# Local attention in a hybrid decoder kernel: values stationary in two column halves, normalised probabilities streamed, the result born transposed

## The chip, the cores and the metric

The program runs on one core of a Trainium2 chip. Its time is the device time of one execution in microseconds (us); the time given for a kernel is the median of its runs. The engines are TensorE (PE for matmuls, PEld for the loads of its stationary operand), VectorE (DVE), ScalarE (ACT), GpSimd (POOL) and SyncE (SP, which here only issues DMAs).

## The reference, cut to what matters

Two layers; each is half a feed-forward block, a mixing block with three branches, and half a feed-forward block. All is f32. The branch that is changed is the sliding-window attention: 256 tokens in two blocks of 128, 16 query heads of 64 columns, 2 key/value heads.

```python
def sliding_window_attention(q, k, v, sinks):
    ...
    s = jnp.einsum('bnqkgd,bnskd->bnkgqs', qb, kk,
                   preferred_element_type=jnp.float32) * (hd ** -0.5)
    ...
    m = jnp.maximum(jnp.max(s, axis=-1, keepdims=True), sink)
    p = jnp.exp(s - m)
    p = p / (jnp.sum(p, axis=-1, keepdims=True) + jnp.exp(sink - m))
    o = jnp.einsum('bnkgqs,bnskd->bnqkgd', p.astype(v.dtype), vv)
    return o.reshape(B, S, H * hd)
```

The result is multiplied with `w_up_swa` (1024 x 1024), gated and added to the other two branches.

## The kernel before, in words

Weights come from HBM in units of 1 MB (128 partitions x 2048 f32). A unit lands in a raw buffer; ACT rounds it to a high part `w_hi` (line 1171), DVE subtracts to get the low part `w_lo` (line 1566), and PE multiplies in three passes, low-high, high-high and high-low (lines 763 to 765), 24 matmuls of 512 columns for a unit. There are three slots of `w_hi`/`w_lo` (`RING`), so ACT may split a unit only when PE is through with the one three items back. Some matrices are multiplied in pairs with a scheme of seven block products (`rk:5`, `rg:1` and so on, 12 matmuls each), for which sums of weight quarters are made either by DVE (line 1563, "raw") or by a DMA of POOL that adds on landing (line 700, table `ADDED`).

The order of everything in the mixing block is one list, `SCHEDULE`, and all engines walk it. `mk0.1` is a unit, `rk:5` a block product, the rest are steps. Those of the local attention, for each group `g` of four heads: `s0` to `s3` (scores; PE line 971, then on DVE scale, mask and maximum, lines 1828 to 1839), `e0` to `e3` (exponentials and row sums on ACT, line 1472), `pt0` to `pt3` (12 transposes of probabilities on PE, line 983, copied out by ACT to `pT`, line 1397), `pv0` to `pv3` (probabilities times values). In `pv` the transposed probabilities are stationary and the values, 64 columns, stream (lines 995 and 997); the result is token-major, and DVE divides it by the row sums on its way to the buffer `stA` (line 1853). When all four groups are there, `st` transposes `stA` (16 transposes, line 820), and ACT and DVE make the high and low parts `bT_hi` and `bT_lo` of it (lines 1188 and 1584). These are the stationary operand of the units `us0.0` to `us1.1`.

Raw buffers: three of their own; `raw_x` in the place of `x` while `x` is parked in HBM; and in the mixing block `raw_b`, two units in the place of `bT_hi`/`bT_lo`, from behind the `mv` units until `st` (constant `B_ITEMS`).

PE takes a matmul with f32 operands as two records in the trace (16 for the 8 score matmuls of a group, 24 for the 12 value matmuls). `prob` holds two groups at a time.

Of the kernel before, what the change touches and what calls it, by code (L numbers as in the profile page):

```python
# [189 lines left out]
RAW_B, RAW_Q, RAW_X = (3, 4), (5, 6), 7  # L190
X_ITEMS = AT[0]["mix", UNIT_AT["mk1", 0]] + 4, AT[0]["mix", UNIT_AT["wo0", 0]] - 6
_st = STEPS.index(("step", "st"))
_after_st = next(s for s in STEPS[_st:] if s[0] != "step")
B_ITEMS = (max(AT[0]["mix", UNIT_AT[c, 1]] for c in ("mv0", "mv1")) + 5,
           AT[0][_after_st if _after_st[0] == "prod" else ("mix", _after_st[1])] + 1)
# [104 lines left out]
def plan_banks(l):  # L300
# [38 lines left out]
    sizes |= {f"pt{g}": (3, False) for g in range(NGRP)} | {f"pv{g}": (1, False) for g in range(NGRP)}  # L339
# [1670 lines left out]
```

## Time and profile before

| what | value |
|---|---|
| median of 3 runs | 1453.86 us (1453.58 to 1456.06) |
| the profiled execution's own time | 1452.88 us |
| its span, first to last instruction | 1451.1 us |
| PE busy in the span | 1431.3 us (99%), 6814 matmuls |
| DVE busy | 1162.2 us (80%) |
| ACT busy | 977.7 us (67%) |

The profiled execution took 1452.88 us, 1.8 us more than its span, and 1.0 us less than the median. A busy time counts a matmul from its start to its modelled end, and neighbours overlap; what a matmul costs is therefore read as the distance between two starts.

### The profile page before, as it was taken

The numbers are of one execution on the slowest core, as the hardware profiler recorded it, in microseconds if no ns is written. First come the engines' busy times: TensorE is split into PE (matmuls) and PEld (weight loads), VectorE is DVE, ScalarE is ACT, GpSimd is POOL, SyncE is SP. The second block draws the span as 40 slices with busy tenths as digits, with TensorE's granted clock in tenths as the row PEclk, the third lists the DMA queues.
The fourth block names the chain that finished last, engine by engine and source line by source line (L and its number), as shares of the span: only waits on it lengthen the run. The fifth ranks groups of instructions, "written<-read, shape, count | busy, mean of one in ns | idle before, by whom it ended". The sixth has DMA issues, their size and how long they took to land.

```text
span 1451.1 us, 17969 instructions
## 1 busy us (share of the span) xinstructions
PE 1431.3 (99%) x6814; PEld 1186.6 (82%) x6814; DVE 1162.2 (80%) x1322; ACT 977.7 (67%) x1430; POOL 67.9 (5%) x93
## 2 busy tenths in 40 slices
PE   8999999999999999999999999999999999999997
PEld 6887888888888888888888778888888888888885
DVE  7999756798768768898798986468987778689985
ACT  6777666769756647676577775668696666576763
POOL 0000000000000000000000000000000000000000
PEclk9999999999999999999999999999999999999999
DMA  9998738775668777788849776467865787768871
GB/s 367 267 291 236 276 130 276 243 232 178 173 221 262 219 301 245 238 281 250 300 144 279 251 214 250 196 208 265 234 171 196 229 246 232 307 198 267 259 233 44
DMA packets 49397, 341.42 MB, mean 235 GB/s; under 512 B 5568, under 2 KB 6208, under 8 KB 8608
## 3 DMA queue, kind: packets, MB, share of 16 engines
q1 hardware_dynamic: 37392, 259.54, 47.5%
q0 software_dynamic: 8912, 63.84, 22.9%
q10 hardware_dynamic: 3008, 16.90, 2.9%
q8 instruction: 55, 0.90, 0.2%
q14 instruction: 30, 0.25, 0.0%
HBM read 332.91 MB, written 7.34 MB: 234 GB/s over the span
## 4 chain that ended last, share of the span: by engine, by line
PE 83%; DVE 10%; DMA 3%; issue 2%; ACT 1%; SPq 0%; POOLq 0%; POOL 0%; DVEq 0%; ACTq 0%
PE bank L763 25%; PE bank L765 24%; PE bank L764 24%; DVE w_lo L1566 5%; PE bank L820 3%; DMA raw_b<-in_stream 3%; DVE w_lo_more L1566 2%; PE bank L997 1%; PE bank L1098 1%; PE bank L1080 1%; PE bank L971 1%; PE bank L983 1%; DMA raw<-in_stream 1%; DVE raw L1563 1%; PE bank L995 0%
## 5 line engine op out<-in xcount | busy, mean ns | idle before, releaser
L1566 DVE TENSOR_TENSOR w_lo<-raw,w_hi 128x1024 fp32r<-128x1024 f32 x342 | 402.3, 1219 | 133.4 <-ACT w_hi L1171 133.2
L1171 ACT ACTIVATE w_hi<-raw 128x1024 fp32r<-128x1024 f32 x342 | 342.9, 1053 | 168.2 <-PE bank L765 136.1
L763 PE MATMUL bank<-w_hi,hT_lo 128*128 128x512 f32 (+1 forms) x696 | 274.3, 394 | 2.7 <-DVE half L1669 1.9
L765 PE MATMUL bank<-w_lo,hT_hi 128*128 128x512 f32 (+1 forms) x696 | 268.3, 386 | 0.0
L764 PE MATMUL bank<-w_hi,hT_hi 128*128 128x512 f32 (+1 forms) x696 | 267.9, 385 | 0.0
L763 PEld LDWEIGHTS bank<-w_hi,hT_lo 128*128 128x128 f32 x696 | 130.9, 188 | 32.1 <-DVE half L1669 2.8
L765 PEld LDWEIGHTS bank<-w_lo,hT_hi 128*128 128x128 f32 x696 | 130.8, 188 | 26.7
L764 PEld LDWEIGHTS bank<-w_hi,hT_hi 128*128 128x128 f32 x696 | 131.1, 188 | 24.4
L763 PE MATMUL bank<-w_hi,S_lo 128*128 128x512 f32 x364 | 144.9, 398 | 1.3 <-ACT snap L1252 0.9
L765 PE MATMUL bank<-w_lo,S_hi 128*128 128x512 f32 x364 | 142.1, 390 | 0.0
L764 PE MATMUL bank<-w_hi,S_hi 128*128 128x512 f32 x364 | 141.9, 390 | 0.0
L1566 DVE TENSOR_TENSOR w_lo<-raw_b,w_hi 128x1024 fp32r<-128x1024 f32 x96 | 113.0, 1217 | 21.4 <-ACT w_hi L1171 21.2
L763 PE MATMUL bank<-w_hi,bT_lo 128*128 128x512 f32 x320 | 125.5, 392 | 0.0
L765 PE MATMUL bank<-w_lo,bT_hi 128*128 128x512 f32 x320 | 124.7, 390 | 0.0
L764 PE MATMUL bank<-w_hi,bT_hi 128*128 128x512 f32 x320 | 124.6, 389 | 0.0
L1171 ACT ACTIVATE w_hi<-raw_b 128x1024 fp32r<-128x1024 f32 x96 | 96.3, 1055 | 36.0 <-PE bank L765 24.5
L763 PE MATMUL bank<-w_hi,gT_lo 128*128 128x512 f32 x240 | 94.5, 394 | 3.6 <-DVE gT_lo L1584 3.5
L765 PE MATMUL bank<-w_lo,gT_hi 128*128 128x512 f32 x240 | 93.6, 390 | 0.0
L764 PE MATMUL bank<-w_hi,gT_hi 128*128 128x512 f32 x240 | 93.5, 389 | 0.0
L1566 DVE TENSOR_TENSOR w_lo<-raw_q,w_hi 128x1024 fp32r<-128x1024 f32 x72 | 84.7, 1218 | 4.6 <-ACT w_hi L1171 4.5
L1171 ACT ACTIVATE w_hi<-raw_q 128x1024 fp32r<-128x1024 f32 x72 | 72.3, 1056 | 15.8 <-PE bank L765 12.3
L763 PEld LDWEIGHTS bank<-w_hi,S_lo 128*128 128x128 f32 x364 | 68.4, 188 | 17.7 <-ACT snap L1252 1.6
(227 smaller groups left out, 2436.3 us busy)
## 6 DMA issues: line engine op xcount, KB each, us to landing
raw<-in_stream SPq DMA_DIRECT2D x150, 1024.0 KB, 6.1
raw_b<-in_stream SPq DMA_DIRECT2D x38, 1024.0 KB, 6.7
raw_q<-in_stream SPq DMA_DIRECT2D x38, 1024.0 KB, 6.9
raw<-in_stream POOLq DMA_DIRECT2D x34, 1024.0 KB, 9.0
raw_x<-in_stream SPq DMA_DIRECT2D x18, 1024.0 KB, 6.8
raw_b<-in_stream POOLq DMA_DIRECT2D x16, 1024.0 KB, 10.8
raw_q<-in_stream POOLq DMA_DIRECT2D x8, 1024.0 KB, 9.3
raw<-in_stream SPq DMA_DIRECT2D x8, 256.0 KB, 7.1
```

What stands on the lines that cost most here:

```text
L763: nc.tensor.matmul(dst, xl, wh[:, a:b], start=first, stop=False, skip_group_check=more)
L764: nc.tensor.matmul(dst, xh, wh[:, a:b], start=False, stop=False, skip_group_check=more)
L765: return nc.tensor.matmul(dst, xh, wl[:, a:b], start=False, stop=last, skip_group_check=more)
L820: last = nc.tensor.transpose(bank(name)[:, at:at + P], src(t, k0 + j), ident[:, :])
L971: last = nc.tensor.matmul(bank(name)[:, i * n:(i + 1) * n], sqT[rows, head // 2, tokens(b)], skT[rows, head // (SWA_H // SWA_KV), 0:n], st ...
L983: last = nc.tensor.transpose(bank(name)[:, i * P:(i + 1) * P], prob[:, g % 2, head, col:col + P], ident[:, :])
L997: last = nc.tensor.matmul(o[:, HD:2 * HD], pT[:, GRP + 2 * i + t, :], v[t], start=t == 0, stop=t == TT - 1)
L1080: last = nc.tensor.matmul(bank(name)[:, t * MEM:(t + 1) * MEM], mqT[:, 2 * h + k, tokens(t)], mkT[:, 2 * h + k, :], start=k == 0, stop=k == 1)
L1098: last = nc.tensor.matmul(bank(name)[:, j * SEQ:(j + 1) * SEQ], mv[:, m, k * P:(k + 1) * P], mpT[:, h, m, :], start=m == 0, stop=m == 1)
L1171: nc.scalar.activation(slots(o)[0][:, part], raw_slot(s)[:, part], ACT.Copy).then_inc(hi_split, 1)
L1563: nc.vector.tensor_tensor(raw_slot(to[0]), raw_slot(to[0]), raw_slot(plus[0]), ALU.add).then_inc(weights_made, 1)
L1566: nc.vector.tensor_tensor(lo[:, part], raw_slot(s)[:, part], hi[:, part].bitcast(F32), ALU.subtract)\
```

## The change

The value product is turned round. The values of a key/value head (128 tokens x 64) are stationary and the transposed probabilities of the group stream. Even heads go to partitions 0 to 63 of the bank and odd heads to partitions 64 to 127, so the bank holds two heads per 128 rows, already transposed. Per group there are 4 matmuls (two of 512 columns for the first block of keys, two of 256 for the second) in the place of 12. Since rows are now columns, the division by the row sums can't come behind: DVE normalises the probabilities before they are transposed, in new steps `n0` to `n3`, and `pt` waits for them. The bank of `pv` goes straight to `bT_hi` (ACT) and `bT_lo` (DVE), and the step `st` with its transposes is gone. `us0.0` waits for `pv0` and `pv1`, `us0.1` for `pv2` and `pv3`.

As `bT` is written from `pv0` on, `raw_b` can be lent only until then. `stA` is free from the end of `mkt` to the first `mq` unit; in it a new raw buffer `raw_a` (one unit) is lent. The lists of orders, `S_AFTER` and `ADDED` are others.

```diff
-mk0.1+xt0 mk1.0+xt1 mk1.1 sq1.0 skv.0 mkt ... s0 rk:5 mv1.0 e0 s1 rk:3 mv1.1 rk:1 e1 pt0 rv0.0 rk:6 pv0 pt1 rk:7 rk:2 s2 mv_out ...
+mk0.1+xt0 mk1.0+xt1 skv.0 mk1.1 sq0.0 ... rk:5 s0 mv0.1 rk:3 e0 s1 mv1.0 mv1.1 e1 n0 n1 rk:1 rv0.0 pt0 rk:6 pv0 pt1 rk:7 mv_out rk:2 s2 ...
...
-S_AFTER = {(0, 1): (1, 2, 3), (0, 2): (0, 1, 2), (1, 1): (0, 1, 3), (1, 2): (0, 1, 2)}
+S_AFTER = {(0, 1): (0, 2, 3), (0, 2): (0, 1, 2), (1, 1): (0, 1, 4), (1, 2): (0, 1, 2)}
...
-RAW_B, RAW_Q, RAW_X = (3, 4), (5, 6), 7
+RAW_B, RAW_Q, RAW_X, RAW_A = (3, 4), (5, 6), 7, 8
...
+B_ITEMS = max(AT[0]["mix", UNIT_AT[c, 1]] for c in ("mv0", "mv1")) + 5, item_after("pv0") + 1
+A_ITEMS = item_after("mkt") + 4, MQ_ITEM + 1
...
                 def grp_transposes(g):
-                    pe.wait_ge(swa_exp, l * NGRP + (g + 1))
+                    pe.wait_ge(swa_probs, l * NGRP + (g + 1))
...
-                    for i in range(GRP):
-                        v = [sv[:, t, kv * HD:(kv + 1) * HD] for t in range(TT)]
-                        o = bank(name)[:, 2 * i * HD:2 * (i + 1) * HD]
-                        nc.tensor.matmul(o[:, 0:HD], pT[:, i, :], v[0], start=True, stop=True)
-                        for t in range(TT):
-                            last = nc.tensor.matmul(o[:, HD:2 * HD], pT[:, GRP + 2 * i + t, :], v[t],
-                                                    start=t == 0, stop=t == TT - 1)
+                    heads = pT[:, :, :].rearrange("p (j o c) q -> p j o c q", j=2, o=2)
+                    for t in range(TT):
+                        v = sv[:, t, kv * HD:(kv + 1) * HD]
+                        for odd in range(2):
+                            o = bank(name)[odd * HD:(odd + 1) * HD, :].rearrange("p (j b q) -> p j b q", j=2, b=TT)
+                            if t == 0:
+                                nc.tensor.matmul(o, v, heads[:, :, odd, 0:2, :], start=True, stop=False, skip_group_check=True)
+                            else:
+                                last = nc.tensor.matmul(o[:, :, 1, :], v, heads[:, :, odd, 2, :], start=False, stop=True,
+                                                        skip_group_check=True)
...
-                    elif s == "st":
-                        wait_out(l, [f"pv{g}_0" for g in range(NGRP)], ["st_0"])
-                        for j in range(4):
-                            transpose_to(l, f"st_{j}", token_major(stA), 2 * j)
...
+                    elif s in ("pv0", "pv1", "pv2", "pv3"):
+                        if s == "pv0" and PAIRS[0]:
+                            act.wait_ge(weights_made, last_read(l, RAW_B, *B_ITEMS))
+                        hi_parts(l, f"{s}_0", bT_hi, 2 * int(s[2]), None)
...
-                        name = f"pv{g}_0"
-                        dve.wait_ge(*full(l, name))
-                        for t in range(TT):
-                            o = bank(name)[:, :].rearrange("p (h b d) -> p h b d", h=GRP, b=2)[:, :, t, :]
-                            dst = stA[:, t, GRP * HD * g:GRP * HD * (g + 1)].rearrange("p (h d) -> p h d", h=GRP)
-                            i = nc.vector.tensor_tensor(dst, o, ssum[:, par, :, t:t + 1].broadcast_to([P, GRP, HD]), ALU.mult)
-                        i.then_inc(free(name), 1)
+                        for b, (c0, c1) in enumerate(((0, WIN), (WIN, 3 * WIN))):
+                            i = nc.vector.tensor_tensor(pr[:, :, c0:c1], pr[:, :, c0:c1],
+                                                        ssum[:, par, :, b:b + 1].broadcast_to([P, GRP, c1 - c0]), ALU.mult)
+                        i.then_inc(swa_probs, 1)
+                    elif s in ("pv0", "pv1", "pv2", "pv3"):
+                        lo_parts(l, f"{s}_0", bT_hi, bT_lo, 2 * int(s[2]), None)
```

The steps of the order that the prediction speaks of, engine by engine. PE in layer 0, before: the value product of group 0 (`sv` streams, `pT` stationary) and the first of what follows.

```order
1180 L995 MATMUL bank<-sv,pT 128x64
1181 L997 MATMUL bank<-sv,pT 128x64 x2
1182 L995 MATMUL bank<-sv,pT 128x64
1183 L997 MATMUL bank<-sv,pT 128x64 x2
1184 L995 MATMUL bank<-sv,pT 128x64
1185 L997 MATMUL bank<-sv,pT 128x64 x2
1186 L995 MATMUL bank<-sv,pT 128x64
1187 L997 MATMUL bank<-sv,pT 128x64 x2
```

PE at the same place after the change, from the end of the product `rk:6` to the transposes of group 1.

```order
1177 L777 MATMUL bank<-w_hi,S_lo 128x512
1178 L778 MATMUL bank<-w_hi,S_hi 128x512
1179 L779 MATMUL bank<-w_lo,S_hi 128x512
1180 L1012 MATMUL bank<-pT,sv 64x512 x2
1181 L1014 MATMUL bank<-pT,sv 64x2x128 x2
1182 L997 MATMUL bank<-ident,prob 128x128 x12
```

The 12 matmuls became 4, on 64 partitions each; what stands around them is as it was.

DVE in layer 0, before, from the scores of group 1 (`smax`) to the division of group 0 (`stA`).

```order
142 L1839 TENSOR_TENSOR ssink<-gains,smax 128x8
143 L1566 TENSOR_TENSOR w_lo<-raw,w_hi 128x1024 x2
144 L1566 TENSOR_TENSOR w_lo<-raw_x,w_hi 128x1024 x2
145 L1566 TENSOR_TENSOR w_lo<-raw,w_hi 128x1024 x2
146 L1563 TENSOR_TENSOR raw_x<-raw_x,raw 128x2048
147 L1566 TENSOR_TENSOR w_lo<-raw,w_hi 128x1024 x2
148 L1776 SCALAR_TENSOR_TENSOR stB<-bank,minus_rstd,stB 128x512
149 L1563 TENSOR_TENSOR raw_b<-raw_b 128x2048
150 L1566 TENSOR_TENSOR w_lo<-raw_x,w_hi 128x1024 x2
151 L1844 TENSOR_TENSOR ssum<-ssum,sexp 128x8
152 L1846 RECIPROCAL ssum<-ssum 128x8
153 L1853 TENSOR_TENSOR stA<-bank,ssum 128x256 x2
```

DVE at the same place after the change.

```order
142 L1858 TENSOR_TENSOR ssink<-gains,smax 128x8
143 L1585 TENSOR_TENSOR w_lo<-raw,w_hi 128x1024 x4
144 L1863 TENSOR_TENSOR ssum<-ssum,sexp 128x8
145 L1865 RECIPROCAL ssum<-ssum 128x8
146 L1868 TENSOR_TENSOR prob<-prob,ssum 128x4x128
147 L1868 TENSOR_TENSOR prob<-prob,ssum 128x4x256
148 L1863 TENSOR_TENSOR ssum<-ssum,sexp 128x8
149 L1865 RECIPROCAL ssum<-ssum 128x8
150 L1868 TENSOR_TENSOR prob<-prob,ssum 128x4x128
151 L1868 TENSOR_TENSOR prob<-prob,ssum 128x4x256
152 L1585 TENSOR_TENSOR w_lo<-raw,w_hi 128x1024 x2
153 L1585 TENSOR_TENSOR w_lo<-raw_a,w_hi 128x1024 x2
```

The normalisations of groups 0 and 1 stand together behind the splits of two units, where the division of group 0 stood behind those of five; the split for `rk:7` and what follows comes after them.

ACT after the change, from the exponentials' end in `e1` to the copy of `pv0`.

```order
161 L1395 ACTIVATE stB<-bank,rstd 128x512
162 L1184 ACTIVATE w_hi<-raw 128x1024 x2
163 L1184 ACTIVATE w_hi<-raw_a 128x1024 x2
164 L1414 ACTIVATE pT<-bank 128x512 x3
165 L1184 ACTIVATE w_hi<-raw 128x1024 x2
166 L1201 ACTIVATE bT_hi<-bank 128x512
```

Two splits of weights now stand between `e1` and the copies of `pt0`, where the copies stood directly behind `e1`.

## Rows read from the trace of the kernel before

**Rows 1.** The page: busy shares; clock by slice; chain by engine.

```profile
PE 1431.3 (99%) x6814; PEld 1186.6 (82%) x6814; DVE 1162.2 (80%) x1322; ACT 977.7 (67%) x1430; POOL 67.9 (5%) x93
...
PEclk9999999999999999999999999999999999999999
...
PE 83%; DVE 10%; DMA 3%; issue 2%; ACT 1%; SPq 0%; POOLq 0%; POOL 0%; DVEq 0%; ACTq 0%
```

**Rows 2.** The page's costliest groups: busy, mean ns of one | idle before, releaser.

```profile
L763 PE MATMUL bank<-w_hi,hT_lo 128*128 128x512 f32 (+1 forms) x696 | 274.3, 394 | 2.7 <-DVE half L1669 1.9
...
L763 PE MATMUL bank<-w_hi,S_lo 128*128 128x512 f32 x364 | 144.9, 398 | 1.3 <-ACT snap L1252 0.9
...
L763 PE MATMUL bank<-w_hi,gT_lo 128*128 128x512 f32 x240 | 94.5, 394 | 3.6 <-DVE gT_lo L1584 3.5
```

**Rows 3.** Timeline of PE: start, length; around the scores of group 0.

```profile
256.41 0.39 PE L764 MATMUL bank<-w_hi,bT_hi 128*128 128x512 f32 x1
256.64 0.39 PE L765 MATMUL bank<-w_lo,bT_hi 128*128 128x512 f32 x1
256.96 1.58 PE L971 MATMUL bank<-skT,sqT 64*128 64x128 f32 x16
258.47 0.50 PE L763 MATMUL bank<-w_hi,S_lo 128*128 128x512 f32 x1
258.80 0.40 PE L764 MATMUL bank<-w_hi,S_hi 128*128 128x512 f32 x1
```

**Rows 4.** Timeline of PE: value product of group 0, transposes of group 1.

```profile
288.67 0.39 PE L765 MATMUL bank<-w_lo,S_hi 128*128 128x512 f32 x1
288.90 0.33 PE L995 MATMUL bank<-sv,pT 128*128 128x64 f32 x2
...
291.52 1.48 PE L983 MATMUL bank<-ident,prob 128*128 128x128 f32 x12
292.76 0.47 PE L763 MATMUL bank<-w_hi,S_lo 128*128 128x512 f32 x1
```

**Rows 5.** Timeline of PE: the step `st` of layer 0.

```profile
374.25 1.91 PE L820 MATMUL bank<-ident,stA 128*128 128x128 f32 x16
375.92 0.48 PE L763 MATMUL bank<-w_hi,hT_lo 128*128 128x512 f32 x1
```

**Rows 6.** Timeline of PE: f32 matmuls of 256 columns, memory attention.

```profile
489.19 7.07 PE L1098 MATMUL bank<-mpT,mv 128*128 128x256 f32 x32
495.90 0.58 PE L763 MATMUL bank<-w_hi,hT_lo 128*128 128x512 f32 x1
```

**Rows 7.** Groups by line and shape, all of the span.

```profile
L1890 DVE TENSOR_TENSOR mprob<-mprob,msum 128x512 f32<-128x512 f32 x8 | 5.5, 692 | 0.3
...
L1566 DVE TENSOR_TENSOR w_lo<-raw,w_hi 128x1024 fp32r<-128x1024 f32 x342 | 402.3, 1219 | 133.4 <-ACT w_hi L1171 133.2
...
L1853 DVE TENSOR_TENSOR stA<-bank,ssum 128x256 f32<-128x256 f32 x16 | 6.0, 419 | 0.5 <-DVE ssum L1846 0.2
...
L1584 DVE TENSOR_TENSOR bT_lo<-bank,bT_hi 128x512 fp32r<-128x512 f32 x16 | 10.3, 684 | 2.8 <-ACT bT_hi L1188 2.8
...
L1563 DVE TENSOR_TENSOR raw<-raw 128x2048 f32<-128x2048 f32 x13 | 29.7, 2284 | 6.5 <-DMA raw<-in_stream 6.5
```

**Rows 8.** Busy time by engine, from the scores to `st`, layer 0.

```profile
258.50:374.40 115.90, 115.90 (x624) 97.54 (x623) 104.29 (x139) 91.51 (x162) 5.17 (x6) 1.00 0.72 216
```

**Rows 9.** Timeline of ACT around `e1` and the copies of `pt0`.

```profile
276.43 1.25 ACT L1323 ACTIVATE mv_made<-bank,rstd_mem 128x512 f32<-128x512 f32 x2
...
280.16 2.00 ACT L1171 ACTIVATE w_hi<-raw 128x1024 fp32r<-128x1024 f32 x2
282.06 0.19 ACT L1468 ACTIVATE sexp<-ssink 128x8 f32<-128x8 f32 x1
...
285.67 1.54 ACT L1397 ACTIVATE pT<-bank 128x512 f32<-128x512 f32 x3
```

**Rows 10.** DMA issues: KB each, median us from issue to landing.

```profile
raw<-in_stream SPq DMA_DIRECT2D x150, 1024.0 KB, 6.1
```

More of the change, by code:

```diff
@@ L76 @@
 SCHEDULE = """
-mk0.1+xt0 mk1.0+xt1 mk1.1 sq1.0 skv.0 mkt S_sum S_hi S_lo sq0.0 skt sq0.1 sq1.1 mv0.0 sqt mv0.1 s0 rk:5 mv1.0 e0 s1 rk:3 mv1.1 rk:1 e1 pt0 rv0.0 rk:6 pv0 pt1 rk:7 rk:2 s2 mv_out rk:4 rg:5 e2 pv1 rotq rv0.1 s3 rg:1 rv1.0 rg:3 rotk pt2 rg:6 rqt rv1.1 e3 rkt pv2 rg:2 rg:7 mq1.0 rg:4 gs:5 pt3 gs:1 gs:3 rs gs:6 pv3 gs:2 st mq1.1 gs:7 ro re gs:4 gr:1 us0.0 us0.1 mq0.0 mq0.1 us1.0 gr:5 mqt mkT_in gr:3 us1.1 rt gr:6 gr:2 gr:7 ur0.0 ur0.1 gr:4 gm:5 ms me mv_in gm:1 ur1.0 mn gm:3 ur1.1 mpt gm:6 mpv gm:2 gm:7 um0.0 gm:4 x_in um0.1 um1.0 mg0 um1.1 wo0.0 mg1 wo1.0 wo0.1 wo1.1+yt0
+mk0.1+xt0 mk1.0+xt1 skv.0 mk1.1 sq0.0 S_sum S_hi S_lo mkt sq0.1 sq1.0 skt sq1.1 mv0.0 sqt rk:5 s0 mv0.1 rk:3 e0 s1 mv1.0 mv1.1 e1 n0 n1 rk:1 rv0.0 pt0 rk:6 pv0 pt1 rk:7 mv_out rk:2 s2 rk:4 rg:5 pv1 e2 n2 rotq rv0.1 s3 rv1.0 rg:3 rqt rg:1 pt2 e3 rotk rg:6 rg:2 pv2 rv1.1 rg:7 n3 mq1.0 rkt rg:4 gs:5 pt3 gs:3 rs gs:1 gs:2 pv3 mq1.1 gs:6 ro gs:7 re us0.0 gs:4 us0.1 mq0.0 gr:1 gr:5 mq0.1 us1.0 mqt us1.1 rt mkT_in gr:3 gr:6 gr:2 ur0.0 gr:7 ur0.1 gr:4 ms gm:5 me mv_in ur1.0 mn gm:3 gm:1 ur1.1 mpt gm:6 mpv gm:7 gm:2 um0.0 gm:4 um0.1 um1.0 x_in mg0 um1.1 wo0.0 mg1 wo1.0 wo0.1 wo1.1+yt0
 """.split()
@@ L187, in quarter_unit, with item_after @@
     return unit_of(("up", f, PAIRS[f][k][int(q[1]) - 1], int(q[0]) - 1))
-RAW_B, RAW_Q, RAW_X = (3, 4), (5, 6), 7
+RAW_B, RAW_Q, RAW_X, RAW_A = (3, 4), (5, 6), 7, 8
 X_ITEMS = AT[0]["mix", UNIT_AT["mk1", 0]] + 4, AT[0]["mix", UNIT_AT["wo0", 0]] - 6
[L192 to L195, printed above, removed]
+def item_after(name):
+    s = next(s for s in STEPS[STEPS.index(("step", name)):] if s[0] != "step")
+    return AT[0][s if s[0] == "prod" else ("mix", s[1])]
+B_ITEMS = max(AT[0]["mix", UNIT_AT[c, 1]] for c in ("mv0", "mv1")) + 5, item_after("pv0") + 1
+MQ_ITEM = AT[0]["prod", 0, "mq", 5] if "mq" in PAIRS[0] else min(AT[0]["mix", UNIT_AT[c, 1]] for c in ("mq0", "mq1"))
+A_ITEMS = item_after("mkt") + 4, MQ_ITEM + 1
 def raw_slots(o):
@@ L207, in raw_slots @@
         slots += RAW_B
+    if PAIRS[0] and A_ITEMS[0] < i < A_ITEMS[1]:
+        slots.append(RAW_A)
     return slots
@@ L338, in plan_banks @@
     sizes |= {f"s{g}": (4, False) for g in range(NGRP)}
[L339 removed]
+    sizes |= {f"pt{g}": (3, False) for g in range(NGRP)} | {f"pv{g}": (1, True) for g in range(NGRP)}
     live, turned = {}, 1
@@ L406, in build @@
         gfin = new("gfin", [P, D], at=a_at)
+        raw_a = new("raw_a", [P, UW], at=a_at)
         stB, b_at = place("stB", [P, TT, D])
@@ L662, in _ @@
                     sp.wait_ge(*full(o // NI, "mv1t1"))
+                if s == RAW_A and (owner is None or o // NI != owner // NI):
+                    sp.wait_ge(*full(o // NI, "mkt_3"))
                 if s == RAW_X and (owner is None or o // NI != owner // NI):
@@ L1839, in step @@
                         nc.vector.tensor_tensor(ssink[:, par], sink, smax[:, par], ALU.subtract).then_inc(swa_max, 1)
-                    elif s in ("pv0", "pv1", "pv2", "pv3"):
-                        g = int(s[2])
-                        par = g % 2
+                    elif s in ("n0", "n1", "n2", "n3"):
+                        g = int(s[1])
+                        pr, par = prob[:, g % 2], g % 2
                         dve.wait_ge(swa_exp, l * NGRP + (g + 1))
```

38 lines of the change are left out of this document (21 added, 17 removed).

## The prediction

> **What bounds the kernel now.** I read the shares of busy time first, then the waits, then single starts. PE is busy 99% of the span, its granted clock is at the full level in all slices, and the chain that ended last lies on PE for 83% [rows 1]. The idle time that PE spends on somebody is small: 2.7, 1.3 and 3.6 us before the three kinds of weight matmul that carry it [rows 2]. So nearly all of the time is what PE is given to do, and a change is worth what it takes from PE, less what it makes PE wait. A matmul of 512 columns starts 0.23 us after the one before it (256.41 to 256.64), though its record is 0.39 us long [rows 3]; costs on PE are therefore distances between starts. DVE is the engine to watch: 80% over all, but 104.29 of 115.90 us in the stretch from the scores to `st` (the columns are the stretch, its length, then busy PE, PEld, DVE, ACT, POOL, the clock, the DMA share, GB/s) [rows 8].
>
> **What is removed: `st`.** Its 16 transposes take from 374.25 to 375.92, 1.67 us [rows 5]. It stands once in each layer: 3.3 us less. It was on PE's line of work with nothing beside it, so all of it counts. The high and low parts that ACT and DVE made behind it are made behind `pv` instead, four of each as before.
>
> **What is exchanged: the value product.** Before, one takes from 288.90 to 291.52, 2.62 us for 24 records, 0.109 us each [rows 4]. A record of the transposes that follow, of 128 columns, takes 0.103 us (291.52 to 292.76 for 12), so a record that streams 64 columns costs no less than one of 128: these 24 pay for loading 128 stationary columns, not for streaming.
>
> After, there are 8 records: four of 512 and four of 256 columns. The price of an f32 record by its columns is in the memory attention: 32 of 256 columns from 489.19 to 495.90, 0.210 us each [rows 6], so I take 0.42 us for 512. In a row that is 4 x 0.42 + 4 x 0.21 = 2.52 us, hardly less than 2.62. The gain hangs on whether the two column halves of the array work at once. No row has such a matmul. The nearest are the scores, which use the two halves of the array's rows in turn, 64 rows each: 8 records of 128 and 8 of 256 columns, in a row 8 x 0.105 + 8 x 0.21 = 2.52 us, and they take from 256.96 to 258.47, 1.51 us [rows 3]. That agrees with a simple rule: the two records of one matmul follow each other, and the first record of the next matmul, on the other half, runs beside the second of this one. It gives four steps of 0.105 and five of 0.21, 1.47 us. The same rule for the new product: three steps of 0.42 and two of 0.21, 1.68 us.
>
> Going in and out of the halves costs something: the scores start 0.32 us after the matmul ahead, and the second matmul behind them starts 0.33 us after the first, where 0.23 is usual [rows 3]; so 0.1 us at each end. The Trainium skill ("TensorEngine Tiling (Array Packing)", Key Properties) says that a change of tiling mode drains TensorE; by that rule these two gaps are the drain, and the new product has them too.
>
> The new product is then 1.68 + 0.2 = 1.88 us, 0.74 less than 2.62, and for eight products 5.9 us less. The bounds: no overlap at all, 2.72 us, which is 0.8 us more for eight; full overlap, 1.26 + 0.2 = 1.46 us, 9.3 us less for eight. I take 1.88, since the scores are built in the same way and alternate in the same way.
>
> One rule speaks against it. The Trainium skill ("TensorE: Matmul & The Clock Gate", Part 3, What overlaps and what doesn't) has weight loads overlap with running matmuls only when their row groups differ, and two column halves share all rows; the same part gives 2.38 times for three column tiles. By the rule alone the product would take the 2.72 us of the row without overlap or more, by the measured tiles about 1.5.
>
> **What is added on DVE.** Each group gets two multiplications in place, of 512 and 1024 elements per partition. The like one of `mprob` takes 0.692 us for 512, and a subtraction of 1024 takes 1.219 [rows 7]: 1.91 us for a group, 7.6 for a layer. The division into `stA` goes, 2 x 0.42 x 4 = 3.4 us. The four low parts, 0.684 each, 2.7 us, now fall into the stretch. One sum of weight quarters, 2.28 us [rows 7], goes from DVE to a DMA of POOL (`ADDED` for `rk` gets a 4). So 104.3 + 7.6 - 3.4 + 2.7 - 2.3 = 108.9 us of DVE in the stretch. PE's stretch: the order takes `mv0.1` into it and `rk:5` out, 12 matmuls or 2.7 us more, which is only moved, and the products give back 4 x 0.74 = 3.0: 115.6 us. DVE still fits, with 6.7 us free where it had 11.6. On the sum: 0. If that cover were gone, what DVE is late with next are the `w_lo` of the units behind, for which PE waits.
>
> **New waits.** `pt` now waits for `n`, and `n` for `e`. The tight place is `e1 n0 n1 rk:1 rv0.0 pt0 rk:6 pv0`. Let T be the end of `mv1.1` on PE. PE then has `rk:1` (2.7), `rv0.0` (5.4), `pt0` (1.3), `rk:6` (2.7), and wants `pv0` at T + 12.1. ACT: the last copy of `mv` and a split until T + 2.8, `e1` 3.6 us (282.06 to 285.67) until 6.4, a copy and the split for `rk:7` until 9.0, one more split until 11.0, the three copies of `pt0` 1.5 us [rows 9] until 12.5. PE waits 0.4 us, in each layer. On DVE `n0` and `n1` end near T + 8.8; behind them are the halves of `w_lo` for `rk:7`, which ACT has ready at 9.0 and PE wants after `pv0` and `pt1`, at T + 15.7: in time. Groups 2 and 3 have three or more items between `n` and `pt`. I take 0.8 us for these and 0.2 for the rest: 1.0 us.
>
> **Buffers.** `raw_b` (two units) is no longer there from `rk` to `gs`, `raw_a` (one) is, from `mkt` to `mq`. By the list of loads, a buffer is free at least three items ahead of its use, where before it was two at the worst place. Three items are 8.2 us or more, a landing takes 6.1 [rows 10]. SP and POOL have the same number of loads in each layer but for POOL's one more at `rk` and one less in the last pair of the second feed-forward. 0. The other orders of the feed-forwards move single items by one place; the weight work is the same. PE's waits there are all that they could win, and the three of [rows 2] are 7.6 us in both layers together; 0, with 3 us either way.
>
> **The sum**, against the profiled execution: 1452.9 - 3.3 - 5.9 + 1.0 = 1444.7 us (its span 1451.1 becomes 1442.9). The median of the runs is 1.0 us above that execution: 1445.7.
>
> **The rivals.** What a measurement of this kernel can tell from no change is about 0.2%, 2.9 us.
>
> (a) The sum as it stands, overlap as in the scores: 1443 to 1448.
>
> (b) The column halves don't overlap. For it: no row shows them doing so. Against it: the scores. 1453.9 - 3.3 + 0.8 + 1.0 = 1452.4.
>
> (c) DVE starves PE: `n` stands at the head of DVE and waits for exponentials while `w_lo` queue behind it. If DVE keeps the 11.6 us of idle time that it had in the stretch, and half of the three places (`n1`, `n2`, `n3`) cost a full `e` of 3.6 us, 5.4 us more, the stretch is 108.9 + 17.0 = 125.9 us instead of 115.6, 10.3 more a layer: 1445.7 + 20.6 - 1.0 = 1465. It is slower by 0.2% once DVE's idle time in the stretch passes 12.7 us a layer ((1456.8 - 1444.7) / 2 = 6.1 more than 115.6). Against it: most of the 11.6 us is slack, since PE didn't wait there.
>
> (d) The change does what it says, but more small waits than I counted at `pv` and `pt`, or in the new orders, eat 2 to 6 us of it: 1448 to 1452.
>
> (e) The new orders also take 2 to 4 us from PE's waits: 1442 to 1443.
>
> **How the numbers follow.** Chances: (a) 0.56, (b) 0.15, (c) 0.09, (d) 0.12, (e) 0.08. The likeliest is (a), 1445.7. The range from 1441.5 to 1452.5 leaves out (c) and the edges of the others, and takes in full overlap (1442.3) and none (1452.4). Faster by over 0.2% means below 1451.0: (a), (e) and most of (d), 0.74. Within 0.2%: (b) and the rest of (d), 0.17. Slower: (c), 0.09.
>
> **What would show it.** Right: 1.7 to 1.9 us from the first value matmul to the next block's start, with 0.32 us ahead of it; no transposes of `stA` but those of `mkt` and `mqt`; multiplications of `prob` of 0.69 and 1.2 us; PE's busy share as before over a span near 1443; DVE near 109 us from `s0` to `pv3`. Wrong: a value product of 2.5 us or more is (b); PE idle before a weight matmul, released by `w_lo`, between `e1` and `pv3`, with DVE waiting for `prob` ahead of it, is (c); waits for the DMA of `raw_a` or of POOL's sums would mean that the buffers, which I set at nothing, have a price.

## The result and the profile after

The changed kernel takes 1439.11 us, median of 4 runs (1438.86 to 1440.71); the kernel before, in the same series, 1453.89 us (1453.58 to 1456.06). The ratio is 0.9897, 95% interval 0.988 to 0.9915: 1.0% faster, 14.8 us. Forecast were 1445.7 us and a range down to 1441.5, so the direction was right, the gain too small, 8.2 us where 14.8 came, and the measured time lies below the range. The profiled execution took 1440.71 us with a span of 1438.8, against 1452.88 and 1451.1 before.

The page of the changed kernel, beside [rows 1] and [rows 2]: busy shares, clock, chain by engine, then the three weight groups that carry PE's waits (busy, mean ns | idle before, releaser) and the new buffer's loads.

```profile
PE 1418.9 (99%) x6654; PEld 1165.2 (81%) x6654; DVE 1169.9 (81%) x1322; ACT 973.3 (68%) x1426; POOL 67.9 (5%) x93
...
PEclk9999999999999999999999999999999999999999
...
PE 87%; DVE 7%; DMA 3%; ACT 2%; issue 1%; POOL 0%; POOLq 0%; DVEq 0%; ACTq 0%
...
L777 PE MATMUL bank<-w_hi,hT_lo 128*128 128x512 f32 (+1 forms) x684 | 268.0, 392 | 3.1 <-DVE half L1688 1.4
...
L777 PE MATMUL bank<-w_hi,S_lo 128*128 128x512 f32 x372 | 148.6, 400 | 1.2 <-ACT snap L1265 1.2
...
L777 PE MATMUL bank<-w_hi,gT_lo 128*128 128x512 f32 x248 | 97.5, 393 | 1.1 <-DVE gT_lo L1603 1.0
...
raw_a<-in_stream SPq DMA_DIRECT2D x12, 1024.0 KB, 6.3
```

The span is 12.3 us shorter, and PE's busy time fell by 12.4 (1431.3 to 1418.9). Its idle time is 19.9 us (1438.8 less 1418.9) and was 19.8. The gain is work taken from PE; waits neither ate much of it nor shrank much.

Where in the program it came is read from two marks that both kernels have on PE, the first transpose of `x` ahead of the mixing block and the first behind it. PE's timeline in layer 0, before:

```profile
199.00 0.27 PE L820 MATMUL bank<-ident,x 128*128 128x128 f32 x1
...
546.89 0.27 PE L820 MATMUL bank<-ident,x 128*128 128x128 f32 x1
```

and after:

```profile
199.29 0.27 PE L834 MATMUL bank<-ident,x 128*128 128x128 f32 x1
...
540.99 0.27 PE L834 MATMUL bank<-ident,x 128*128 128x128 f32 x1
```

347.9 us became 341.7, 6.2 less; in layer 1 the same marks give 348.1 and 341.6, 6.5 less. All feed-forwards together are 0.4 us longer. One mixing block differs by up to some 1 us from one execution to the next: in the profile of `e0`, a later run of the same kernel, the two take 341.7 and 342.8.

Now the value product. PE's timeline of group 1, which no transposes follow, before (start, length):

```profile
305.27 0.39 PE L765 MATMUL bank<-w_lo,S_hi 128*128 128x512 f32 x1
305.50 0.33 PE L995 MATMUL bank<-sv,pT 128*128 128x64 f32 x2
...
308.09 0.48 PE L763 MATMUL bank<-w_hi,hT_lo 128*128 128x512 f32 x1
308.41 0.39 PE L764 MATMUL bank<-w_hi,hT_hi 128*128 128x512 f32 x1
```

and the same product after:

```profile
304.69 0.39 PE L779 MATMUL bank<-w_lo,S_hi 128*128 128x512 f32 x1
305.01 1.08 PE L1012 MATMUL bank<-pT,sv 128*64 128x512 f32 x4
305.92 0.60 PE L1014 MATMUL bank<-pT,sv 128*64 128x256 f32 x4
306.45 0.50 PE L777 MATMUL bank<-w_hi,hT_lo 128*128 128x512 f32 x1
306.79 0.40 PE L778 MATMUL bank<-w_hi,hT_hi 128*128 128x512 f32 x1
```

From the last matmul ahead to the second behind it was 3.14 us (305.27 to 308.41) and is 2.10 (304.69 to 306.79): 1.04 us less for this product. The same distances of all eight products sum to 24.5 us before and 16.7 after, 7.9 us less: four give 1.04 each. The two of group 0 give 0.92, since after the change they start 0.1 us late, and the two of group 2 give 0.93, since before they stood only 0.11 us behind transposes. The product itself takes 1.44 us (305.01 to 306.45), where 1.68 was forecast. The gap of 0.33 behind it, which I counted as a price of the halves, is nothing new: it was 0.32 (308.09 to 308.41) behind the old product too, and is 0.34. Only the gap ahead grew much, from 0.23 to 0.32.

Rows of PE's timeline merge neighbours of one shape. Asked for a stretch of 0.02 to 0.05 us, it shows only the records that run in it. For group 0, asked at 289.44, at 290.40 and at 290.80:

```profile
289.45 0.65 PE L1012 MATMUL bank<-pT,sv 128*64 128x512 f32 x2
...
289.90 0.63 PE L1012 MATMUL bank<-pT,sv 128*64 128x512 f32 x2
290.33 0.41 PE L1014 MATMUL bank<-pT,sv 128*64 128x256 f32 x2
...
290.54 0.41 PE L1014 MATMUL bank<-pT,sv 128*64 128x256 f32 x2
```

The records go in pairs, the two halves at the same time: pairs of 512 columns from 289.45 and 289.90, pairs of 256 from 290.33 and 290.54, and the block that follows starts at 290.89. That is full overlap of the two halves: 0.45 and 0.43 us for the pairs of 512, 0.21 for the first of 256, and 0.35 for the last, which has some 0.14 of an end in it. I read a pair as one record of each half, and not as the two of one matmul. On the full array the records come one after the other, 0.109 us apart [rows 4], and in `e3` below the trace has two pairs of 512 in a row, though one half's 512 and 256 columns are issued there before the other's.

The other engines. DVE, ACT and the rest in layer 0 from 0.6 us ahead of the scores of group 0 to the start of the last value product (the third busy time is DVE's; [rows 8] begins behind the scores and ends at `st`, so the two stretches are alike but not the same):

```profile
254.00:366.50 112.50, 112.46 (x569) 89.38 (x569) 101.42 (x137) 88.94 (x163) 6.04 (x7) 1.00 0.78 225
```

The new steps in the groups by shape:

```profile
L1603 DVE TENSOR_TENSOR bT_lo<-bank,bT_hi 128x512 fp32r<-128x512 f32 x16 | 10.6, 683 | 0.6 <-ACT bT_hi L1201 0.6
L1868 DVE TENSOR_TENSOR prob<-prob,ssum 128x1024 f32<-128x1024 f32 x8 | 9.7, 1218 | 0.0
...
L1868 DVE TENSOR_TENSOR prob<-prob,ssum 128x512 f32<-128x512 f32 x8 | 5.5, 692 | 0.3
```

The multiplications cost 1.218 and 0.692 us, as forecast. DVE is idle for 11.1 us of the stretch, where 6.7 were forecast. It makes two sums of weight quarters in it, where it made four in that of [rows 8] and I took off one, and 50 halves of `w_lo`, where it made 52; that is 2.3 and 2.4 us of the 7.5 by which its work is less than the 108.9 forecast.

### The profile page after: what moved, and what is told of

Same layout as the page of the kernel before. It is cut to its first block, busy times and chain, and to the rows that moved or that the text cites. A ratio compares the mean times of both kernels' runs of the same rounds, so it can differ in the third digit from the quotient of the medians.

```text
span 1438.8 us, 17632 instructions
## 1 busy us (share of the span) xinstructions
PE 1418.9 (99%) x6654; PEld 1165.2 (81%) x6654; DVE 1169.9 (81%) x1322; ACT 973.3 (68%) x1426; POOL 67.9 (5%) x93
## 4 chain that ended last, share of the span: by engine, by line
PE 87%; DVE 7%; DMA 3%; ACT 2%; issue 1%; POOL 0%; POOLq 0%; DVEq 0%; ACTq 0%
PE bank L777 26%; PE bank L779 26%; PE bank L778 26%; DVE w_lo L1585 4%; PE bank L834 3%; DMA raw_b<-in_stream 2%; DVE w_lo_more L1585 1%; PE bank L1111 1%; PE bank L1093 1%; PE bank L985 1%; DMA raw<-in_stream 1%; PE bank L997 1%; PE bank L1012 1%; ACT w_hi L1184 1%; PE bank L768 0%
## 5 line engine op out<-in xcount | busy, mean ns | idle before, releaser
L1585 DVE TENSOR_TENSOR w_lo<-raw,w_hi 128x1024 fp32r<-128x1024 f32 x338 | 397.7, 1219 | 122.6 <-ACT w_hi L1184 122.0
L1184 ACT ACTIVATE w_hi<-raw 128x1024 fp32r<-128x1024 f32 x338 | 339.0, 1054 | 145.9 <-PE bank L779 132.0
L777 PE MATMUL bank<-w_hi,hT_lo 128*128 128x512 f32 (+1 forms) x684 | 268.0, 392 | 3.1 <-DVE half L1688 1.4
L779 PE MATMUL bank<-w_lo,hT_hi 128*128 128x512 f32 (+1 forms) x684 | 263.4, 385 | 0.0
L778 PE MATMUL bank<-w_hi,hT_hi 128*128 128x512 f32 (+1 forms) x684 | 263.2, 385 | 0.0
L777 PE MATMUL bank<-w_hi,S_lo 128*128 128x512 f32 x372 | 148.6, 400 | 1.2 <-ACT snap L1265 1.2
L1585 DVE TENSOR_TENSOR w_lo<-raw_q,w_hi 128x1024 fp32r<-128x1024 f32 x78 | 91.8, 1218 | 5.0 <-ACT w_hi L1184 5.0
L1184 ACT ACTIVATE w_hi<-raw_q 128x1024 fp32r<-128x1024 f32 x78 | 78.3, 1056 | 24.6 <-PE bank L779 17.6
L779 PEld LDWEIGHTS bank<-w_lo,S_hi 128*128 128x128 f32 x372 | 69.8, 188 | 15.0
L778 PEld LDWEIGHTS bank<-w_hi,S_hi 128*128 128x128 f32 x372 | 70.0, 188 | 13.8
```

The lines of the kernel that those rows point to most:

```text
L777: nc.tensor.matmul(dst, xl, wh[:, a:b], start=first, stop=False, skip_group_check=more)
L778: nc.tensor.matmul(dst, xh, wh[:, a:b], start=False, stop=False, skip_group_check=more)
L779: return nc.tensor.matmul(dst, xh, wl[:, a:b], start=False, stop=last, skip_group_check=more)
L1184: nc.scalar.activation(slots(o)[0][:, part], raw_slot(s)[:, part], ACT.Copy).then_inc(hi_split, 1)
L1585: nc.vector.tensor_tensor(lo[:, part], raw_slot(s)[:, part], hi[:, part].bitcast(F32), ALU.subtract)\
```

## The experiments

Each runs beside the kernel before on the same chip, and ratios are to it. The changed kernel without an edit, run again, is the base of the differences (`e0`).

> The changed kernel once more, beside the kernel before on the same chip, for the ratio and a second profile. Both theories: 0.988 to 0.9915 of before, a span of 1437 to 1439 us.

1440.22 us (4 runs), ratio 0.9901 (0.9886 to 0.9916). Intervals of this width, 0.15% to either side, are 2 us, and smaller differences between two medians are read as none.

**The transposes of `st`, put back (`e1`).** The last group transposes 16 times more in each layer.

```diff
-                        for i in range(4):
+                        for i in (list(range(4)) * (3 if j < 2 else 1) if g == 3 else range(4)):
```

> The changed kernel with 16 transposes more in each layer (those of the probabilities of group 3 into their first two banks are made three times), as many as the step st had. Theory W (PE's work sets the time, a record costs its distance between starts): 16 x 0.104 = 1.7 us a layer, 3.3 us more than the changed kernel. Theory O (PE's work is partly hidden, and new orders made the gain): under 1.5 us more.

1444.07 us, ratio 0.9929 (0.9917 to 0.9942): 3.9 more than `e0`, where 3.3 was expected from the trace. `st` was paid in full. In this run's trace the two mixing blocks are 5.5 us longer than the changed kernel's, and 1.5 us of that are two waits for `gates` that the changed kernel's profile doesn't have.

**The value product, twice (`e2`).**

```diff
-                    for t in range(TT):
+                    for t in (0, 1, 0, 1):
```

> The changed kernel with every value product made twice into the same bank. If the two column halves work at once throughout (records start in pairs), one more product is 2 x 0.42 + 2 x 0.21 = 1.26 us, eight are 10.1 us more. By the staggered rule of the prediction one more is 1.68 us, eight 13.4 us more. With no overlap 2.52 us, 20.2 us more.

1450.87 us (7 runs), ratio 0.9974 (0.9964 to 0.9985): 10.7 more than `e0`, or 1.33 for each of eight products. PE's timeline of this kernel, group 0:

```profile
288.52 1.08 PE L1012 MATMUL bank<-pT,sv 128*64 128x512 f32 x4
289.40 0.63 PE L1014 MATMUL bank<-pT,sv 128*64 128x256 f32 x4
289.84 1.06 PE L1012 MATMUL bank<-pT,sv 128*64 128x512 f32 x4
290.69 0.63 PE L1014 MATMUL bank<-pT,sv 128*64 128x256 f32 x4
```

The first takes 1.32 us (288.52 to 289.84). Full overlap (1.26) is right; my staggered rule (1.68) and no overlap (2.52) are not.

**The halves in another order (`e3`).** Each half finishes before the other begins, so that matmuls of different halves are neighbours only once.

```diff
-                    for t in range(TT):
-                        v = sv[:, t, kv * HD:(kv + 1) * HD]
-                        for odd in range(2):
+                    for odd in range(2):
+                        for t in range(TT):
+                            v = sv[:, t, kv * HD:(kv + 1) * HD]
```

> The changed kernel with the four matmuls of a value product in another order: both of the even heads, then both of the odd heads. If overlap needs matmuls on different halves side by side, only the two in the middle can share time: 0.42 + 0.21 + 0.42 + 0.21 in halves, at least 2.52 - 0.42 = 2.1 us and at most 2.52, so 5 to 9 us more than the changed kernel for eight. If PE finds the pairs by itself in its queue: no more than 0.5 us.

1439.62 us, ratio 0.9899 (0.9886 to 0.9913): no change. PE's timeline asked at 289.60 and at 290.44 shows the same pairs as before the edit, though the program now issues 512, 256, 512, 256 columns:

```profile
289.55 0.66 PE L1012 MATMUL bank<-pT,sv 128*64 128x512 f32 x2
...
290.00 0.64 PE L1012 MATMUL bank<-pT,sv 128*64 128x512 f32 x2
290.43 0.42 PE L1014 MATMUL bank<-pT,sv 128*64 128x256 f32 x2
```

**The orders of the feed-forwards, as before (`e4`)**: their lists, `S_AFTER`, and their part of `ADDED`.

```diff
-S_AFTER = {(0, 1): (0, 2, 3), (0, 2): (0, 1, 2), (1, 1): (0, 1, 4), (1, 2): (0, 1, 2)}
+S_AFTER = {(0, 1): (1, 2, 3), (0, 2): (0, 1, 2), (1, 1): (0, 1, 3), (1, 2): (0, 1, 2)}
```

> The changed kernel with the orders of the feed-forward blocks, S_AFTER and the feed-forward part of ADDED as before. Theory W: within 1 us of the changed kernel, since PE's waits there were small. Theory O: 2 to 5 us more.

1440.28 us, ratio 0.9908 (0.9895 to 0.992): nothing.

**`raw_a` taken away (`e5`)**, but for one item.

```diff
-A_ITEMS = item_after("mkt") + 4, MQ_ITEM + 1
+A_ITEMS = MQ_ITEM, MQ_ITEM + 1
```

> The changed kernel without the lent buffer raw_a: four raw buffers in the mixing block from rk to gs instead of five. Theory W: loads are early enough by three items, 0 to 1 us more. Theory O: PE waits for splits that wait for landings, over 3 us more.

1473.36 us, ratio 1.0129 (1.0116 to 1.0142): 33 us slower than `e0`, and slower than the kernel before. Waits in this kernel from 280 to 400 us (total, times, longest):

```profile
ACT w_hi L1184 <- DMA raw_x<-in_stream: 15.4, 2, 8.8
PE bank L1012 <- DVE sdec L1878: 5.5, 1, 5.5
...
PE bank L985 <- DVE bT_lo L1603: 4.7, 2, 4.4
```

ACT waits for landings, DVE is late behind it with all that it has, and PE waits for DVE. The page of this run gives PE 1429.3 us busy for the same 6654 matmuls, 10.4 more than the changed kernel; the other 22.4 of the 32.8 us by which the span grew are idle time. The next run shows what such a growth of busy time is.

**The mixing block in the order of before (`e6`)**, with `n0 n1` behind `e1`, `n2` behind `e2`, `n3` behind `e3`, without `st`, and with its part of `ADDED` as before.

```diff
-... rk:5 s0 mv0.1 rk:3 e0 s1 mv1.0 mv1.1 e1 n0 n1 rk:1 rv0.0 pt0 rk:6 pv0 pt1 rk:7 mv_out ...
+... mv0.1 s0 rk:5 mv1.0 e0 s1 rk:3 mv1.1 rk:1 e1 n0 n1 pt0 rv0.0 rk:6 pv0 pt1 rk:7 rk:2 s2 ...
```

> The changed kernel with the order of the mixing block as before (SCHEDULE and its part of ADDED), st taken out and each n put in right behind its e. Theory W: the gain is in PE's work, so it stays, at most 2 us more than the changed kernel. Theory O: 4 us more or above, PE waiting for the probabilities (pt stands right behind n0 and n1).

1476.85 us, ratio 1.0156 (1.0143 to 1.0169): 36.6 slower than `e0`. PE's waits over the whole span:

```profile
PE bank L997 <- DVE prob L1868: 12.6, 2, 6.3
PE bank L777 <- DVE srg L1795: 7.8, 2, 4.2
PE bank L985 <- DVE bT_lo L1603: 4.3, 2, 2.1
```

These three, twice each, are 24.7 us. Its page gives PE 1430.2 us busy for the same 6654 matmuls, 11.3 more than the changed kernel: 24.7 + 11.3 = 36.0, the 35.8 us by which the span grew. The 11.3 are the clock: over the span PE is busy for 22.5 us at a granted clock of 0.50, and half of that is 11.2. (3.4 of the 22.5 lie in the first feed-forward, from 29.8 to 33.2 us, which the edit doesn't reach.) Busy times from the start of the wait for `n1` on (PE's is the first; the granted clock is the third number from the end):

```profile
279.70:282.00 2.30, 0.01 (x1) 0.00 (x0) 2.08 (x3) 2.30 (x4) 0.00 (x0) 1.00 0.88 353
282.00:284.00 2.00, 0.00 (x0) 0.00 (x0) 1.97 (x4) 2.00 (x10) 0.00 (x0) 0.59 0.18 74
284.00:286.00 2.00, 0.00 (x0) 0.00 (x0) 1.96 (x4) 1.93 (x10) 0.00 (x0) 0.50 0.54 123
286.00:288.00 2.00, 1.99 (x10) 1.99 (x11) 1.93 (x4) 0.60 (x1) 0.00 (x0) 0.50 0.97 401
288.00:289.00 1.00, 1.00 (x5) 0.96 (x5) 1.00 (x2) 0.73 (x2) 0.00 (x0) 0.50 0.01 0
289.00:290.00 1.00, 1.00 (x5) 0.80 (x4) 1.00 (x1) 0.47 (x1) 0.00 (x0) 0.91 0.00 0
```

PE's timeline, its first work behind that wait:

```profile
286.01 2.82 PE L997 MATMUL bank<-ident,prob 128*128 128x128 f32 x12 [6.30 <-DVE prob L1868]
```

While PE waits the clock falls to its lower level (0.50 of 2.4 GHz), and it is full again only some 3 us after the work resumed; the 12 transposes take 2.48 us to the next start (286.01 to 288.49), where they took 1.24 [rows 4]. Behind the like wait in layer 1 (6.3 us, until 1013.57) the clock stays at 0.50 for 6 us of work, until 1019.6.

**`pt0`, `pv0` and `pt1` moved in that order (`e10`)**, behind `rv0.0 rk:6`.

```diff
-... e1 n0 n1 pt0 rv0.0 rk:6 pv0 pt1 rk:7 ...
+... e1 n0 n1 rv0.0 rk:6 pt0 rk:7 pv0 pt1 ...
```

> The kernel with the mixing order of before (that ran 36 us over the changed one), with pt0, pv0 and pt1 moved behind rv0.0 and the products rk:6 and rk:7. PE waited 6.5 us a layer ahead of pt0 for the probabilities. If that wait is the place of pt alone: 10 to 15 us less than that kernel, with 20 us still over the changed one from other places. If DVE or the buffers were the bound, the wait only moves: under 4 us less.

1472.13 us, ratio 1.0124 (1.0111 to 1.0138): 4.7 less than `e6`, between what the two theories said. The wait ahead of `pt0` is gone, and PE waits elsewhere, over the whole span:

```profile
PE bank L777 <- DVE stB L1795: 8.5, 2, 4.2
PE bank L777 <- DVE srg L1795: 7.8, 2, 4.2
PE bank L985 <- DVE bT_lo L1603: 4.3, 2, 2.1
```

One late step was not the cause; DVE is late at three places in a layer, whichever step asks. The use of `raw_a` changes with the order as well: 6 loads and 6 adding DMAs of POOL in the old order (here and in `e6`), from which ACT makes 28 halves of `w_hi`, and 12 loads and 24 halves in the new one. It is not used less, but each load is held for more. Whether `e6` loses by that in part what `e5` loses isn't shown.

**Only the table of sums for the mixing block as before (`e14`)**, in the new order.

```diff
-ADDED = {... (0, 'gs'): (6, 7), ... (0, 'rk'): (6, 7, 4), ...}
+ADDED = {... (0, 'gs'): (7, 4), ... (0, 'rk'): (6, 7), ...}
```

> The changed kernel with the mixing block's part of ADDED as before: the sum for rk's product 4 by DVE instead of a DMA of POOL, and for gs product 6 by DVE and 4 by DMA. It splits the 36 us that the mixing order and table of before cost together. If the table is the cause: 10 us more or above; if the order of the steps is: under 2 us more, since DVE has slack.

1444.86 us (5 runs), ratio 0.9935 (0.9923 to 0.9947): 4.6 more than `e0`, again between the theories. If the two add, the table is some 5 of the 36.6 us of `e6` and the order of the steps the rest; the old order with the new table wasn't run.

**More DVE work (`e7`)** at the place of the new one: a maximum of `prob` with itself behind each division, 15.2 us in all.

```diff
+                        for c0, c1 in ((0, WIN), (WIN, 3 * WIN)):
+                            i = nc.vector.tensor_tensor(pr[:, :, c0:c1], pr[:, :, c0:c1], pr[:, :, c0:c1], ALU.max)
```

> The changed kernel with the work of each normalisation on DVE done twice (a maximum of the probabilities with themselves behind it): 7.6 us more of DVE in the attention stretch of each layer, against about 11 us that are free there. If DVE's slack covers: under 1 us more. If DVE is at its limit (rival c): 5 us or more, with PE idle released by w_lo.

1450.2 us (12 runs), ratio 0.9974 (0.9966 to 0.9983): 10 us slower than `e0`.

**Less DVE work (`e9`)**: the multiplications left out.

```diff
-                        for b, (c0, c1) in enumerate(((0, WIN), (WIN, 3 * WIN))):
-                            i = nc.vector.tensor_tensor(pr[:, :, c0:c1], pr[:, :, c0:c1], ...
+                        nc.vector.tensor_scalar(ssum[:, par], ssum[:, par], 1.0, None, ALU.mult).then_inc(swa_probs, 1)
```

> The changed kernel without the two multiplications of each normalisation (the reciprocal is made, the probabilities are not divided): 7.6 us less of DVE in each layer's attention stretch, and pt released that much earlier. If DVE's work is hidden in the changed kernel: within 1 us of it. If it already costs PE something, as the doubled one did: 2 to 5 us less.

1440.76 us, ratio 0.9908 (0.9895 to 0.9922): nothing gained. The 15.2 us that the changed kernel has are hidden, the next 15.2 are not. Busy times in the same stretch, of `e7` and of `e9` (DVE third):

```profile
254.00:366.50 112.50, 108.87 (x549) 85.62 (x548) 104.09 (x135) 86.19 (x159) 6.04 (x7) 1.00 0.75 212
```

```profile
254.00:366.50 112.50, 112.44 (x570) 89.22 (x570) 96.22 (x133) 89.42 (x162) 5.45 (x7) 1.00 0.79 225
```

In `e7` DVE still has 8.4 us of idle time in it, and PE already has 3.6. Between the marks each mixing block of `e7` takes 346.2 us, 4.5 and 4.6 more than in the changed kernel, so the cost stands where the work was added.

**One sum more by DMA (`e11`)**, in `gs`.

```diff
-(0, 'gs'): (6, 7)
+(0, 'gs'): (6, 7, 4)
```

> The changed kernel with one more sum of weight quarters made by an adding DMA of POOL (pair gs, product 4), 2.3 us less of DVE in each layer. Both theories: within 1 us of the changed kernel, since PE doesn't wait there; if better, it is the best version yet.

1440.26 us, ratio 0.99 (0.9884 to 0.9915): nothing.

**The exchange alone, undone (`e8`)**: twelve matmuls of 64 columns in the changed kernel, with the stationary operand of 128 columns as before.

```diff
+                    for i in range(GRP):
+                        v = [sv[:, t, kv * HD:(kv + 1) * HD] for t in range(TT)]
+                        o = bank(name)[:, 2 * i * HD:2 * (i + 1) * HD]
+                        nc.tensor.matmul(o[:, 0:HD], pT[:, 3 * i, :], v[0], start=True, stop=True)
+                        ...
```

> The changed kernel with the value product of before: 12 matmuls of 64 columns with the probabilities stationary, into the same bank and with the same steps around it (the layout of the bank is then not what the next step takes it for; only the time is read). It isolates the exchange. Theory W: 2.62 against 1.44 + 0.2 us, 0.98 each, 7.8 us more than the changed kernel. By the staggered rule of the prediction, 0.74 each: 5.9 us more.

1448.51 us (5 runs), ratio 0.9959 (0.9947 to 0.9972): 8.3 more than `e0`, and 8.3 more than `e11`, which ran in the same series and is as fast as `e0`. Between the marks its two mixing blocks take 345.9 us each, 8.5 more than the changed kernel's together, and its products by their starts 8.7. That is somewhat more than the 7.9 between the two kernels, since in the new order the old product of group 0 starts late too, 0.45 us behind the matmul ahead, and takes 2.70 us.

**`raw_b` lent for shorter, in the kernel before (`e12`)**: it takes no load in the mixing block, where it took four loads and two adding DMAs in each layer.

```diff
-           AT[0][_after_st if _after_st[0] == "prod" else ("mix", _after_st[1])] + 1)
+           AT[0]["prod", 0, "rk", 7] + 1)
```

> The kernel before with raw_b no longer lent behind pv0, as the change must have it, and nothing else. If buffers have no price while each is free three items ahead (the prediction's step): under 2 us more than the kernel before. If the two buffers are what lets PE run without waits in the rk to gs stretch: 10 us more or above; then the changed order and raw_a had to make up for them.

1453.85 us (10 runs), ratio 1.0002 (0.9992 to 1.0011): nothing. The loan that the change cuts short was worth nothing in the old order. The kernel before in the new order of steps wasn't tried.

## Why the prediction was right, and where it was wrong

**What bounds the kernel** was right: the span fell by 12.3 us and PE's busy time by 12.4, with the granted clock full throughout.

**`st`, 3.3 us**: right; `e1` measured 3.9, within the 2 us that such a difference is known to. The trace gives 3.5: behind each `st` the second weight matmul started 0.32 us after the first, where 0.23 is usual, and that went with it.

**The exchange, 5.9 us**: the failed step. The exchange alone is worth 8.3 us (`e8`), and the two traces have 7.9 between them: 1.04 us for a product at most places instead of 0.74. There are two errors in it. That "the first record of the next matmul, on the other half, runs beside the second of this one" is false: both records of both halves run beside each other, 1.44 us in place of 1.68. And of the "0.1 us at each end" the one behind stood in the kernel before as well. The wrong rule was chosen because it gave the scores' 1.51 us as 1.47. But full overlap, 4 x 0.105 + 4 x 0.21 = 1.26, and some 0.2 us lost besides gives 1.46 and fits as well; one total could not tell them apart. The trace of before could have. PE's timeline of that kernel, asked at 257.00, 257.18 and 258.35:

```profile
256.96 0.38 PE L971 MATMUL bank<-skT,sqT 64*128 64x128 f32 x2
...
256.96 0.49 PE L971 MATMUL bank<-skT,sqT 64*128 64x128 f32 x4
...
258.16 0.38 PE L971 MATMUL bank<-skT,sqT 64*128 64x256 f32 x2
```

Two score records run within 0.05 us of the first start, and two more have started by 257.20: pairs, as in the value product. The last pair starts at 258.16 and the block behind it at 258.47, 0.31 us for 256 columns that cost 0.21. The second pair starts at 257.17, 0.21 us behind the first, where 128 columns cost 0.105. So the 0.2 us are lost at the two ends, and the halves overlap in full between them.

**DVE, 0**: right in its result, by `e9`. The amount was forecast as 108.9 us in 115.6 and is 101.4 in 112.5; 6.7 us free was a fair warning, since 7.6 us more in each layer (`e7`) cost 5.

**New waits, +1.0 us**: wrong in sign as a net. The two products of PE's work, 7.9 and 3.5 us, make 11.4 of the 12.7 that both mixing blocks lost (6.2 and 6.5), so 1.3 us came back besides, where 1.0 was to be spent; the feed-forwards lost 0.4. Most of the 1.3 is one wait in each layer of the kernel before, here that of layer 0:

```profile
441.67 0.39 PE L765 MATMUL bank<-w_lo,hT_hi 128*128 128x512 f32 x1
442.25 0.50 PE L763 MATMUL bank<-w_hi,S_lo 128*128 128x512 f32 x1 [0.19 <-DVE gates L1776]
```

It starts 0.58 us behind its neighbour, and the one behind it another 0.34, where 0.23 is usual: 0.47 us too late, 0.9 in both layers. The changed kernel's profile has no late start there. But that of `e0`, the same kernel, has one in layer 1, with 0.8 us of waiting, so the orders don't give this back in every execution, and what of them gives it isn't isolated: 1.3 is below what two medians tell apart, and the feed-forwards' lists are worth nothing (`e4`). At `pv0` of group 0 PE did wait, 0.43 us from 289.02 to 289.45 where 0.32 is usual, so 0.1 us where I said 0.4.

**Buffers and orders, 0**: right as a net and wrong as a reason. The sum took them as independent of the change and of each other. Taken alone, no `raw_a` costs 33 us, the old order of the mixing block 36.6, its old table of sums 4.6, and the shorter loan of `raw_b` nothing. The new order has room for one unit more from `mkt` to `mq`, and needs it. I read only that the new list of loads was no tighter than the old one, and not what each part was worth.

**The profiled execution against the median.** I added 1.0 us, since the median before was so much above its profiled execution. After, the profiled execution was 1.6 above the median of its runs (1440.71 and 1439.11). Single runs of the kernel before go from 1451.91 to 1456.33 over all series, so one execution says where its median lies to some 2 us only.

The miss of 6.6 us (1445.7 and 1439.1) is thus 2.0 in the exchange, 0.2 in `st` and 2.3 in the waits, less 0.4 in the feed-forwards, which is the 4.0 between 1444.7 and the profiled 1440.7 within rounding; and 2.6 in the step from one execution to the median. No one of them left the range alone: with the exchange put right by itself the sum is 1443.3 to 1443.7, inside it. The exchange is the one whose cause the runs show. Of the waits the trace names 0.9, and for the last 2.6 I can give no cause.

**The rivals.** (b), no overlap, is excluded by `e2` and `e8`. (c), DVE starves PE, didn't occur, but `e6` shows it: with the old order it costs 36 us, where I gave 20.6. The waits are 24.7 of it, and 11.3 are the clock, which falls with them and which the price left out. (d) didn't occur. (e), some microseconds from the orders, is near the truth in its time, but of its reason the trace bears out only some 1 us. The range reached down for full overlap alone, and not for full overlap together with anything else.

## What to carry to other kernels

Before a rule on overlap is fitted to the total of a block, ask the trace for stretches shorter than one record: the starts are there, and two rules that give one total part at once. Where few columns stream past a full stationary operand, exchange the operands: 24 records of 64 columns at 0.109 us each became 8 in two halves, 1.44 us. And a buffer that is lent and an order that uses it are one edit: take each away alone before a cost of nothing is written beside either, and price a wait of some microseconds on PE with the clock that it can lose.

## What the runs showed of the hardware that I had not expected

- Two halves of the array's columns, 64 stationary columns each over the same 128 rows, work fully at once: a pair of 512 columns takes 0.43 to 0.45 us to the next, where twice the 0.210 us of 256 columns [rows 6] is 0.42 for one. The Trainium skill ("TensorE: Matmul & The Clock Gate", Part 3, What overlaps and what doesn't) has weight loads overlap running matmuls only when the row groups differ; these share all rows, and the trace shows no such loss, so here the measurement decides. It doesn't hold on the full array of this kernel either: PEld is busy for 82% and PE for 99% of the span before [rows 1], so loads for all 128 rows run beside matmuls. That could have been held against rival (b) from the start.
- The order in which the halves are written doesn't matter (`e3`): the trace lists the four records of 512 columns ahead of the four of 256 though the program alternates them, and the time is the same. Whether PE issues them so or the records are only listed so, the runs don't tell.
- An idle stretch of 6.3 us on PE lowered its clock to 0.50, and it stayed there for 3 us of work behind it in one layer of `e6` and for 6 us in the other. Stretches of some 2 us did it at one place and not at another. In `e7` one of 2.1 us (292.5 to 294.5) left the clock at 1.00, and one of 2.0 (27.3 to 29.3, in the first feed-forward) was followed by 0.50 from 30.7 to 34.1. In `e6` the wait of 2.1 us for `bT_lo` was followed by it in layer 0 (0.50 from 323.3 to 326.7) and not in layer 1. What decides between them isn't shown.
